# Opening the last feed-forward's buffers ahead of the post norm, and squares that follow each tile's rounding

## What is computed

```python
hx = hx + g2 * swiglu(fx, ffn_w1[i], ffn_w3[i], ffn_w2[i])      # last one of the first block
x = rms_norm(hx, final_norm)
h = rms_norm_2(x, mix_pre_norm)
proj = h @ w_in
...                                                             # delta rule and attention: mixed
x = x + rms_norm_2(mixed, mix_post_norm)
h = rms_norm_2(x, ffn_pre_norm)
f = jnp.square(jax.nn.relu(h @ w_up)) @ w_down
x = x + rms_norm_2(f, ffn_post_norm)
```

## Time and profile before

| | us |
|---|---|
| median of 3 runs | 2428.29 (2426.75 to 2429.38) |
| the profiled execution | 2428.0 |
| its span, from the first to the last instruction | 2426.0 |
| TensorE busy | 2278.4 (94% of the span) |
| VectorE busy | 1156.6 (48%) |
| ScalarE busy | 723.6 (30%) |
| mean granted TensorE clock | 0.967 of full |

### The profile page before, as it was taken

One profiled execution on the slowest core, in us unless ns is written; L12 is line 12 of the kernel. 1 busy time (PEld: TensorE's weight loads), 2 busy tenths in 40 slices (PEclk: granted clock), 3 DMA queues, 4 the chain that ended last, 5 costly groups with the idle time before them and its releaser, 6 DMA issues.

```text
span 2426.0 us, 25735 instructions
## 1 busy us (share of the span) xinstructions
PE 2278.4 (94%) x9888; PEld 1779.9 (73%) x9888; DVE 1156.6 (48%) x1440; ACT 723.6 (30%) x905; POOL 25.6 (1%) x52
## 2 busy tenths in 40 slices
PE   6999999999899999899899999999787986999996
PEld 4868686776688888688688888877657864878875
DVE  7554444435775232526533233378666655332334
ACT  3231121212343222312333222255544223322321
POOL 0000000000000000000000000000000000000000
PEclk7999999999999999999999999999798988999998
DMA  7232323213475222222222322232000001222221
GB/s 302 70 117 86 117 86 118 85 69 117 147 286 208 87 99 91 70 103 87 70 104 86 102 89 89 102 104 87 18 1 13 23 35 36 103 87 95 96 89 50
DMA packets 32748, 232.00 MB, mean 96 GB/s; under 512 B 3761, under 2 KB 4017, under 8 KB 5553
## 3 DMA queue, kind: packets, MB, share of 16 engines
q1 hardware_dynamic: 23904, 171.98, 20.2%
q0 software_dynamic: 6912, 50.33, 5.4%
q10 hardware_dynamic: 1872, 8.86, 1.0%
HBM read 229.06 MB, written 2.10 MB: 95 GB/s over the span
## 4 chain that ended last, share of the span: by engine, by line
PE 89%; DVE 7%; ACT 2%; issue 1%; DMA 1%; DVEq 0%; POOL 0%; ACTq 0%; POOLq 0%
PE PS L454 26%; PE PS L455 25%; PE PS L456 25%; PE PS L577 3%; PE PS L568 2%; DVE rv L1532 1%; PE PS L810 1%; PE PS L919 1%; PE PS L931 1%; PE PS L845 1%; PE PS L930 1%; DMA ada_raw<-ada 1%; DVE w_lo L1437 1%; PE PS L487 0%; DVE rstd L1446 0%
## 5 line engine op out<-in xcount | busy, mean ns | idle before, releaser
L454 PE MATMUL PS<-act_hi,w_hi 128*128 128x512 f32 x1632 | 656.9, 402 | 52.5 <-DVEq L2079 23.5
L1437 DVE TENSOR_TENSOR w_lo<-raw,w_hi 128x2048 fp32r<-128x2048 f32 x162 | 371.1, 2291 | 683.5 <-ACT w_hi L1040 683.4
L455 PE MATMUL PS<-act_lo,w_hi 128*128 128x512 f32 x1632 | 650.2, 398 | 0.0
L456 PE MATMUL PS<-act_hi,w_lo 128*128 128x512 f32 x1632 | 649.3, 398 | 0.0
L1040 ACT ACTIVATE w_hi<-raw 128x2048 fp32r<-128x2048 f32 x162 | 310.3, 1915 | 1128.6 <-PE PS L456 1119.6
L454 PEld LDWEIGHTS PS<-act_hi,w_hi 128*128 128x128 f32 x1632 | 309.7, 190 | 134.0 <-issue 28.7
L455 PEld LDWEIGHTS PS<-act_lo,w_hi 128*128 128x128 f32 x1632 | 309.7, 190 | 77.6 <-issue 2.9
L456 PEld LDWEIGHTS PS<-act_hi,w_lo 128*128 128x128 f32 x1632 | 309.4, 190 | 76.2
L454 PE MATMUL PS<-hid_hi,w_hi 128*128 128x512 f32 (+1 forms) x672 | 266.0, 396 | 0.9 <-ACT sg L1398 0.9
L455 PE MATMUL PS<-hid_lo,w_hi 128*128 128x512 f32 (+1 forms) x672 | 265.4, 395 | 0.0
L456 PE MATMUL PS<-hid_hi,w_lo 128*128 128x512 f32 (+1 forms) x672 | 265.4, 395 | 0.0
(11 more groups left out here) (340 smaller groups left out, 2313.7 us busy)
## 6 DMA issues: line engine op xcount, KB each, us to landing
raw<-slabs SPq DMA_DIRECT2D x162, 1024.0 KB, 4.8
ada_raw<-ada POOLq DMA_DIRECT2D x44, 1024.0 KB, 5.1
early_raw<-ada POOLq DMA_DIRECT2D x4, 1024.0 KB, 21.0
toep<-decay ACTq DMA_DIRECT2D x5, 768.0 KB, 4.2
x<-x_t ACTq DMA_DIRECT2D x1, 2048.0 KB, 9.4
out_t<-x SPq DMA_DIRECT2D x4, 512.0 KB, 2.6
rs<-ctx_t ACTq DMA_DIRECT2D x1, 1024.0 KB, 13.9
con<-consts ACTq DMA_DIRECT2D x1, 770.0 KB, 4.4
```

The source lines that it names most:

```text
L454: pe.matmul(o, w[0], a[0], start=first, stop=False)
L455: pe.matmul(o, w[0], a[1], start=False, stop=False)
L456: return pe.matmul(o, w[1], a[0], start=False, stop=last)
L1437: dve.tensor_tensor(w_lo[:, k % 2, :], raw[:, k % 2, :], w_hi[:, k % 2, :].bitcast(F32), ALU.subtract).then_inc(w_lo_done, 1)
```

## The change

There are two edits. The three increments now stand ahead of the post norm's reciprocal on VectorE (`inverse_root("post2")`). And ScalarE squares each tile of x right behind that tile's rounding, while VectorE adds the square of tile s - 2 behind `act_lo` of tile s - 1; with that, the rounding of slab MIX + 1 stands ahead of the last square, and its `w_lo` behind all eight additions. The rest of the diff only takes helpers apart. No instruction that computes is added or removed.

```diff
-            def in_squares(q, order=range(KT)):
-
-                for s, k in enumerate(order):
-                    act.wait_ge(sq_used, 8 * q + max(s - 1, 0))
-                    act.activation(sq[:, s % 2, :], x[:, k, :], ACT.Square).then_inc(sq_ready, 1)
+            def in_square(q, s, k):
+
+                act.wait_ge(sq_used, 8 * q + max(s - 1, 0))
+                act.activation(sq[:, s % 2, :], x[:, k, :], ACT.Square).then_inc(sq_ready, 1)
...
                     act.activation(act_hi[:, k, :], x[:, k, :], ACT.Copy, scale=in_gain[:, 0, k:k + 1]).then_inc(hi_ready, 1)
-                after_static(MIX - 1)
-                in_squares(nth("final"), FIN)
+                    if s == KT - 1:
+                        after_static(MIX - 1)
+                    in_square(nth("final"), s, k)
...
+            def add_weighted(s):
+
+                add_square("final", s, in_gain[:, 1, FIN[s]:FIN[s] + 1])
...
                     if lot == 3 and s:
                         in_rest("pre2", s - 1, FIN[s - 1], in_gain[:, 0, FIN[s - 1]:FIN[s - 1] + 1])
+                        if s >= 2:
+                            add_weighted(s - 2)
...
                 in_rest("pre2", KT - 1, FIN[-1], in_gain[:, 0, FIN[-1]:FIN[-1] + 1])
+                add_weighted(KT - 2)
+                add_weighted(KT - 1)
                 static_rest(MIX + 1)
-                added("final", lambda k: in_gain[:, 1, k:k + 1], FIN)
...
+                dve.sem_inc(relu_done, 4)
+                dve.sem_inc(sqr_done, 2)
+                dve.sem_inc(h2_lo_done, 2)
                 inverse_root("post2")
...
             if has("all"):
-                dve.sem_inc(relu_done, 4)
-                dve.sem_inc(sqr_done, 2)
-                dve.sem_inc(h2_lo_done, 2)
                 added("ffn2")
```

More of the change, by code:

```diff
@@ L1071, in added_root, with in_squares @@
                 act.activation(dst, PS[:, b, :], func, bias=bias, scale=1.0 / D).then_inc(std_ready, 1)
-            def in_squares(q, order=range(KT)):
-                for s, k in enumerate(order):
-                    act.wait_ge(sq_used, 8 * q + max(s - 1, 0))
-                    act.activation(sq[:, s % 2, :], x[:, k, :], ACT.Square).then_inc(sq_ready, 1)
+            def in_square(q, s, k):
+                act.wait_ge(sq_used, 8 * q + max(s - 1, 0))
+                act.activation(sq[:, s % 2, :], x[:, k, :], ACT.Square).then_inc(sq_ready, 1)
+            def in_squares(q):
+                for k in range(KT):
+                    in_square(q, k, k)
             def shifted(q, shift, dst, width):
@@ L1473, in in_rest, with add_square, added @@
                                          op0=ALU.mult, op1=ALU.subtract).then_inc(lo_ready, 1)
-            def added(name, weight=None, order=range(KT)):
+            def add_square(name, s, weight=None):
                 q = nth(name)
[L1478 to L1489, removed]
+                dve.wait_ge(sq_ready, 8 * q + s + 1)
+                if s:
+                    dve.wait_ge(sq_used, 8 * q + s)
+                if s == 0:
+                    ins = dve.tensor_scalar(std[:, :], sq[:, 0, :], 1.0 if weight is None else weight, None, ALU.mult)
+                elif weight is None:
+                    ins = dve.tensor_tensor(std[:, :], std[:, :], sq[:, s % 2, :], ALU.add)
+                else:
+                    ins = dve.scalar_tensor_tensor(out=std[:, :], in0=sq[:, s % 2, :], scalar=weight, in1=std[:, :],
+                                                   op0=ALU.mult, op1=ALU.add)
+                ins.then_inc(sq_used, 1)
+            def add_weighted(s):
+                add_square("final", s, in_gain[:, 1, FIN[s]:FIN[s] + 1])
+            def added(name):
+                for k in range(KT):
+                    add_square(name, k)
             def make_gain(i, norm_col, scale):
```

## The result

The changed kernel took 2410.59 us in the median of four runs (2409.67 to 2413.09), the kernel before 2427.69: a ratio of 0.993, with a 95% interval of 0.9913 to 0.9948. Five more runs in another session gave 2414.55 (2411.38 to 2416.63) against 2428.62, ratio 0.9943 (0.993 to 0.9957). The forecast was 2413.1, from 2410.5 to 2418.0. The profiled execution of the changed kernel took 2413.09 us, 14.9 less than that of the kernel before. The share of TensorE's busy time is again 94%.

A forecast was written before the change was run, and what follows sets the result against it. TensorE, busy for 94% of the span, was taken as the bound, with time won only at its waits and low clock. 2428.0 - 10.8 - 4.4 = 2412.8, plus 0.3 for the median: 2413.1 us, range 2410.5 to 2418.

The forecast's parts named there:

- The increments: Post norm: TensorE's pair of slab FFN2 follows its input tiles and ends at 2043.65, not 2054.47; gain 10.8 us.
- a gap of up to 2.7 us: Post norm, before tile k = 4, where `w_lo` lies between tiles: TensorE's longest idle, which may lower the clock.
- The rule of the Trainium skill: Paced start in the post norm: short idles between matmul groups swing the clock, making the term 8.5 to 10.8 us.
- The squares: Input projection: interleaving covers the 2.7 us wait before the matmul by ones and avoids the low clock; gain 4.4 us.
- 0.2 late: Input projection: `w_lo` of slab MIX + 1 moves back behind the additions and is ready 0.2 us late.
- 1.98 us for a tile: Input projection: VectorE's three operations of 0.66 us for each tile, in place of two taking 1.32 us.
- The cover of the eighth addition: Input projection: the last addition of squares ends 1.1 us before TensorE is done with the pair.
- table load: Input projection, ScalarE: rival that alternating roundings and squares reload activation tables; they share a set, no chance of its own.
- Slab FFN2 + 2: Behind the post norm: ScalarE's later rounding still leaves its `w_lo` ready 1.3 us before TensorE needs it.
- nothing between them that is fixed in time: Some 450 us between the two places: engines wait only for each other and slabs, so all moves with the start.
- a low clock behind the paced start: Feed-forward rival: term 8.5 to 8.9 us, time about 2415; chance 0.09 together with slab FFN2 + 2 late.
- squares that gain little locally: Input projection rival: late additions and `w_lo` leave 1 to 3.4 us, time 2414 to 2417; chance 0.10.

The follow-up runs named there:

- e3: Kernel before with one line moved: `w_lo` of slab MIX + 1 behind the additions of the squares, no interleaving, no moved increments; 2426.64 us, ratio 0.9994.
- e7: e2 with one more VectorE pass for each of seven tiles while the squares are interleaved, output unchanged; 2425.97 us, ratio 0.9992 to the kernel before.
- e1: Kernel before with only the three increments moved ahead of the post norm's reciprocal, squares as before; 2416.12 us, ratio 0.995.
- e2: Changed kernel with the three increments put back in their old place, so only the squares are interleaved; 2425.77 us, ratio 0.9989 to the kernel before.
- e8: Changed kernel with three more matmuls, 0.7 us, ahead of the pair of slab MIX, results overwritten; 2410.42 us, ratio 0.9929 to the kernel before.
- e9: Changed kernel with six more matmuls, 1.4 us, ahead of the pair of slab MIX; 2413.64 us.
- e5: The changed kernel run again, nothing altered, in another session; 2414.55 us, ratio 0.9943 to the kernel before.
- e4: Kernel before with the three increments put inside the post norm, behind `w_lo` of slab FFN2 + 1; 2417.57 us, ratio 0.9956.

## Why the prediction was right, point by point

- **The increments.** Forecast 10.8 us, measured 10.7 (37.57 to 26.83 between the last sum and slab FFN2 + 1). Each step is in the rows: the start behind the first `act_lo`, 0.43 us a matmul at first and 0.23 then, the longest wait behind `w_lo`, the end 1.5 us after the last tile. I had counted a gap of up to 2.7 us there and thought that the clock may fall; it was 2.24 and the clock stayed. The rule of the Trainium skill that I set against it (TensorE: Matmul & The Clock Gate, "A second HAM failure mode: psum-queue depth-cycling") did not show here: no return to the low clock in 13.2 us with four idle spells. In e3 the clock fell behind an idle of 1.07 us and within one of 1.08; in e7 it stayed full through idles of 0.40, 0.93, 0.27 and 1.08 us. So short idles brought it down in one of these three cases. The paced pair also hides how long the clock stays low at first: 10.2 us behind the last sum in the changed kernel, 6.8 in e1, and the segment is 26.8 us in both. In the old order that shows, 37.6 or 38.7 us, so the same edit is worth 10.7 us beside the kernel before and 11.9 beside e2.
- **The squares.** Forecast 4.4 us, measured 4.6; `w_lo` was ready 0.06 us before its slab started, where I had it 0.2 late, and cost nothing: from the matmul by ones to the end of slab MIX + 1 it takes 12.05 us here and in e8, where `w_lo` has 0.7 us more. 1.98 us for a tile held (1578.10 to 1580.08). The cover of the eighth addition was 1.5 us, not 1.1. ScalarE's alternating roundings and squares had no table load between them; the next one in the trace stands at 1583.93, ahead of the root.
- **Slab FFN2 + 2.** Forecast cover 1.3 us, measured 1.9.
- **The step that failed** is the one between the two terms: "nothing between them that is fixed in time: ... all of that moves with the start". The clock doesn't move with the start. With the squares' 4.6 us won, the delta rule and the attention met 6.8 us more at the low clock and took 2.3 us longer. The prediction put this at nothing. The sum of its terms was 15.2; for the profiled execution it was 4.6 + 10.7 - 2.3 = 13.1 by exact lengths, and 2.0 from the part before slab MIX brought it to the 14.9 measured but for 0.2. That these two, which the forecast didn't have, nearly cancel is luck.
- **Its size.** That two terms right to 0.2 us gave medians 17.1 and 14.1 us under before shows how wide one change's result is here: nine runs of the changed kernel cover 7 us (2409.67 to 2416.63). The mean granted clock of each run goes with it: 0.971 in the three runs from 2409.67 to 2410.76 and in the one at 2411.38, 0.968 in the one at 2416.63. In e2 it was 0.968 in the two runs near 2422 and 0.965 in the three above 2427. The rivals' cases, a low clock behind the paced start or squares that gain little locally, did not happen.

That the middle segment's length is set by its time at the low clock is shown by fourteen profiles, by the matched matmuls, and by e8 and e9, which only put matmuls ahead of it whose results are overwritten. Such matmuls also give VectorE and ScalarE 0.7 or 1.4 us more of a lead, and no run separates this from the shift; the column of the first fall speaks for the shift. Why the clock falls just there, and why each kernel meets nearly the same set in each profile, stays open. Where the low stretches of the unprofiled runs lay, no trace shows.

## What to carry to other kernels

A semaphore that stands for "this buffer is free" should be raised when the buffer is free, not when its stage begins: an instruction that could follow its input tile by tile was held for 23.5 us by an increment queued behind that input. Work that feeds a reduction belongs beside the tile that makes it, as long as the engine that does both keeps up with its consumer; count operations for each tile against the consumer's time and look at the last tile. And a local gain should be read between two fixed instructions, since the rest of the program may take more or less time only because it starts elsewhere under the clock.

## What the runs showed of the hardware

- The same 410 us of program took 410.15, 411.9 or 414.3 us when its start was put off by 0.7, 1.4 or 0 us of matmuls (e8, e9, e5).
- An idle of 2.24 us and three of about 0.5 us left the granted clock at 1.00 in the changed kernel, and so did 0.40, 0.93, 0.27 and 1.08 us in e7; two of 1.07 and 1.08 us, with a matmul by ones between, were followed by 0.43 us a matmul and a granted clock of 0.50 in e3. The length of an idle alone doesn't tell what the clock does.
- A bare increment in VectorE's stream had taken effect by 2029.06, 0.6 and 1.2 us before two vector instructions ahead of it in the program had started (e4). Nothing is lost by that here: the pair that they let start writes banks 0 and 1, whose tiles wait in `facc`, and the next banks are written only after the pair, so after the last `act_lo`. I would not let a bare increment stand for finished work without a wait ahead of it.
